# A norm of q and k cut into two chains, and an embedding norm that reads its statistics a tile ahead

## The reference

```python
# first block, inside attention: 4 heads, each with 2 x 64 features
q = rms_norm(q, g_q) * (HEAD_DK ** -0.5)     # over groups of 64 features
k = rms_norm(k, g_k)
# rms_norm(x, g) = x * rsqrt(mean(x * x) + EPS) * g
lam = exp(sum(lq[0] * lq[1])) - exp(sum(lq[2] * lq[3])) + lam_init
bias = bias_table[t5_buckets(kpos - qpos)]   # added to the scores
# after attention
x = x + gate1 * mix
h2 = rms_norm(x, g_norm2) * (1.0 + scale2) + shift2
# gate1, shift2, scale2 are parts of silu(c) @ w_mod + b_mod

# second block, its first line: a layer norm of every token
h = layer_norm(x, ln_emb_g, ln_emb_b)
```

## Time and profile before

| | |
|---|---|
| time, median of 3 | 2403.66 us (2400.92 to 2405.05) |
| profiled execution | 2396.91 us, span 2394.8 us |
| busy: PE / DVE / ACT / POOL | 90% / 73% / 44% / 7% of the span |
| mean granted TensorE clock | 0.932 of full speed |

### The profile page before, as it was taken

How to read it: one execution, slowest core, us unless ns; L and a number is a source line. 1 busy time by engine, 2 the same in 40 slices (tenths; PEclk the granted TensorE clock), 3 DMA queues, 4 the chain that set the end, 5 groups by cost and what they waited for, 6 DMA issues and landing times. The chain is left out here.

```text
span 2394.8 us, 25614 instructions
## 1 busy us (share of the span) xinstructions
PE 2146.2 (90%) x10172; PEld 1667.9 (70%) x10172; DVE 1744.9 (73%) x1857; ACT 1053.7 (44%) x1190; POOL 165.0 (7%) x122
## 2 busy tenths in 40 slices
PE   5999979999954999999999069999999969899997
PEld 3767824667843888888887047888888647788775
DVE  4565135997467799999997359999999469955737
ACT  4387022774224677777775022112221246522123
POOL 2000000000000011111110000000000000042210
PEclk8999986999976999999999569999999978899999
DMA  9111170001276899999997311121222140332201
GB/s 316 44 36 36 36 286 0 1 1 72 88 277 254 316 403 394 395 393 403 393 393 245 127 44 38 63 79 36 83 102 88 33 153 1 124 114 88 71 1 71
DMA packets 125719, 365.03 MB, mean 152 GB/s; under 512 B 11733, under 2 KB 22893, under 8 KB 125623
## 3 DMA queue, kind: packets, MB, share of 16 engines
q1 hardware_dynamic: 111616, 328.68, 36.1%
q0 software_dynamic: 6336, 21.00, 3.4%
q10 hardware_dynamic: 7670, 14.03, 1.6%
HBM read 324.76 MB, written 38.86 MB: 152 GB/s over the span
## 5 line engine op out<-in xcount | busy, mean ns | idle before, releaser
L2031 DVE SCALAR_TENSOR_TENSOR arena<-arena,vecs 128x1023 f32<-128x1023 f32 (+14 forms) x240 | 304.4, 1268 | 7.1
L1560 DVE TENSOR_TENSOR w_low<-W,w_high 128x2048 fp32r<-128x2048 f32 x96 | 217.0, 2287 | 38.9 <-ACT w_high L1512 38.9
L1928 PE MATMUL Q<-hT_high,w_high 128*128 128x512 f32 (+1 forms) x736 | 227.0, 391 | 5.9 <-DVE ring_low L2074 5.8
L1560 DVE TENSOR_TENSOR w_low<-arena,w_high 128x2048 fp32r<-128x2048 f32 x96 | 218.3, 2290 | 17.7 <-ACT w_high L1512 17.7
L1512 ACT ACTIVATE w_high<-W 128x2048 fp32r<-128x2048 f32 x96 | 184.0, 1919 | 96.6 <-PE Q L1455 65.3
L1928 PE MATMUL Q<-hT_low,w_high 128*128 128x512 f32 (+1 forms) x720 | 222.2, 390 | 0.0
L1928 PE MATMUL Q<-hT_high,ring_low 128*128 128x512 f32 x704 | 217.2, 390 | 0.0
L1512 ACT ACTIVATE w_high<-arena 128x2048 fp32r<-128x2048 f32 x96 | 184.2, 1919 | 74.9 <-PE Q L1455 74.9
L1455 PE MATMUL Q<-w_high,x_high 128*128 128x512 f32 x512 | 160.8, 395 | 2.4 <-DVE x_low L1563 2.4
L1928 PEld LDWEIGHTS Q<-hT_high,w_high 128*128 128x128 f32 (+1 forms) x736 | 135.4, 184 | 39.0 <-DVE ring_low L2074 5.9
L1455 PE MATMUL Q<-w_low,x_high 128*128 128x512 f32 x512 | 158.8, 391 | 0.0
(11 more groups left out here) (430 smaller groups left out, 4295.1 us busy)
## 6 DMA issues: line engine op xcount, KB each, us to landing
W<-in_w_dram SPq DMA_DIRECT2D x48, 2048.0 KB, 13.3
arena<-in_w_dram SPq DMA_DIRECT2D x48, 2048.0 KB, 12.3
W<-in_w_mod_dram SPq DMA_DIRECT2D x12, 2048.0 KB, 9.5
W<-in_w_in_dram SPq DMA_DIRECT2D x12, 2048.0 KB, 8.7
W<-in_w_out_dram SPq DMA_DIRECT2D x6, 2048.0 KB, 9.0
spill<-arena ACTq DMA_DIRECT2D x24, 512.0 KB, 2.6
W<-in_w_in_dram SPq DMA_DIRECT2D x8, 1024.0 KB, 7.7
arena<-in_x_dram SPq DMA_DIRECT2D x4, 1024.0 KB, 17.4
```

The lines of the kernel that those rows point to most:

```text
L1560: nc.vector.tensor_tensor(wl[:], chunk_src(r, j), wh[:].bitcast(F32), ALU.subtract).then_inc(low_v, 1)
L1928: ins = nc.tensor.matmul(Q[rows, 2 * (n % 4) + half, :], w[:, k], x[:, k, HALF * half:HALF * half + HALF], start=k == 0 and w is high and ...
L2031: ins = nc.vector.scalar_tensor_tensor(conf[:, i, j:], u[:, 0:S - j], w, conf[:, i, j:], ALU.mult, ALU.add)
```

## The change

In the block of q and k the 16 rows become two chains of 8 rows (`VECS = 2 * HEADS`), one for q (`g` = 0, partitions 0 to 7) and one for k (`g` = 1, partitions 64 to 71), each with its own sums, root (`root`), reciprocal (`invert`) and spread. The inverse roots are split: ScalarE writes the rounded high part (`high_rows`), VectorE the rest 32 partitions further on (`low_rows`), and one fp32r matmul over both spreads them with a rounded mask; the partitions between are zero. TensorE's list begins with a modulation product, the bias product moves behind the first two sums and the second modulation product, and the norms on VectorE use two bank pairs in place of four. The bias round trip goes to GpSimd's queue. `y_rest` moves to the end; the load of `gain2` and L937's operation move two blocks on, to the block of the output projection.

In the block of the embedding norm the tokens come in 8 DMAs of 0.5 MB, the 20 small loads go to GpSimd's queue, and `stats(t + 1)` is done ahead of the passes of tile `t`, in two sets of statistics; the copy of L1758 and a wait go.

```diff
+        VECS = 2 * HEADS
...
+        def rows_of(g):
+            return slice(DK * g, DK * g + VECS)
+
+        def rest_of(g):
+            return slice(DK * g + 32, DK * g + 32 + VECS)
...
+                for h in range(HEADS):
+                    pool.wait_ge(near_ready, h + 1)
+                    pool.dma_start(bias_rows[h].rearrange("(p n) -> p n", p=P), bias_near[h]).then_inc(bias_sent, 16)
+                pool.wait_ge(bias_sent, 16 * HEADS)
+                for h in range(HEADS):
+                    skewed = bias_rows[h, P:].rearrange("(p n) -> p n", n=HALF - 1)[:, 0:NEAR]
+                    pool.dma_start(bias_all[:, h, 6 * P:6 * P + NEAR], skewed).then_inc(bias_in, 16)
...
+                def next_vector(i):
+                    row_product(i)
+                    if i < 5:
+                        mod_product(pe, unit(pe, U_GATE1 + i + 1), 5)
+
+                def sums(g):
+                    for b in range(HEADS):
+                        n = HEADS * g + b
+                        pe.wait_ge(sq_ready, n + 1)
+                        for half in range(2):
+                            ins = nc.tensor.matmul(Q[rows_of(g), sum_bank[g] + half, :], qk_sum[:, b],
+                                                   tiles(n % 2)[:, HALF * half:HALF * half + HALF],
+                                                   start=b == 0, stop=b == HEADS - 1)
+                        ins.then_inc(sum_mm, 1)
+                        if b % 2:
+                            next_vector(2 * g + b // 2)
+                        if n == 1:
+                            near()
+
+                def spread(g):
+                    pe.wait_ge(parts_low, g + 1)
+                    span = slice(DK * g, DK * g + 32 + VECS)
+                    for b in range(HEADS):
+                        n = HEADS * g + b
+                        if n >= 2:
+                            pe.wait_ge(qk_normed, n - 1)
+                        for half in range(2):
+                            ins = nc.tensor.matmul(Q[:, 6 * (n % 2) + half, :], qk_spread[span, b],
+                                                   qk_parts[span, HALF * half:HALF * half + HALF],
+                                                   start=True, stop=True)
+                        ins.then_inc(spread_mm, 1)
+
+                def near():
+                    pe.wait_ge(hot_in, 16)
...
                 mod_product(pe, unit(pe, U_GATE1), 5)
-                for b in range(8):
-                    pe.wait_ge(sq_ready, b + 1)
-                    for half in range(2):
-                        ins = nc.tensor.matmul(Q[0:VECS, 6 + half, :], qk_sum[:, b],
-                                               tiles(b % 2)[:, HALF * half:HALF * half + HALF],
-                                               start=b == 0, stop=b == 7)
-                    ins.then_inc(sum_mm, 1)
-                    if b % 2:
-                        row_product(b // 2)
-                        mod_product(pe, unit(pe, U_GATE1 + b // 2 + 1), 5)
-                row_product(4)
-                mod_product(pe, unit(pe, U_GATE1 + 5), 5)
+                pe.wait_ge(lam_ready, 1)
+                nc.tensor.matmul(Q[:, 4, 0:2], ones[0:DK, :], lam_pr[0:DK, 0:2], start=True, stop=True)\
+                    .then_inc(lam_mm, 1)
+                pe.wait_ge(masks, 2)
+                sums(0)
+                pe.wait_ge(near_ready, HEADS)
+                sums(1)
+                next_vector(4)
+                pe.wait_ge(masks, 7)
+                pe.wait_ge(mask_ready, 1)
+                spread(0)
                 row_product(5)
-                pe.wait_ge(mod_added, 6)
-                pe.wait_ge(near_ready, HEADS)
-                pe.wait_ge(rows_inv, 1)
-                for b in range(8):
-                    if b >= 4:
-                        pe.wait_ge(qk_normed, b - 3)
-                    for half in range(2):
-                        ins = nc.tensor.matmul(Q[:, 2 * (b % 4) + half, :], qk_spread[:, b],
-                                               qk_rows[:, HALF * half:HALF * half + HALF], start=True, stop=True)
-                    ins.then_inc(spread_mm, 1)
+                spread(1)
...
+                def high_rows(g):
+                    act.wait_ge(rows_inv, g + 1)
+                    nc.scalar.activation(qk_parts[rows_of(g)], qk_rows[rows_of(g)], ACT.Copy).then_inc(parts_high, 1)
...
+                part(1)
+                root(0)
+                square(4)
+                square(5)
+                part(2)
+                square(6)
+                square(7)
+                act.wait_ge(masks, 7)
+                high_rows(0)
+                part(3)
+                root(1)
+                part(4)
                 for m in range(2):
                     nc.scalar.activation(y_high[m][:], y_lru[:, m], ACT.Copy).then_inc(ylru_high_ready, 1)
-                act.wait_ge(sum_mm, 8)
-                nc.scalar.activation(qk_rows, bank2(3)[0:VECS], ACT.Sqrt, bias=eps_col[0:VECS], scale=1.0 / DK)\
-                    .then_inc(root_q, 1)
-                for i in (4, 5):
-                    part(i)
+                part(5)
+                high_rows(1)
...
+                def invert(g):
+                    dve.wait_ge(root_q, g + 1)
+                    nc.vector.reciprocal(qk_rows[rows_of(g)], qk_rows[rows_of(g)]).then_inc(rows_inv, 1)
+
+                def low_rows(g):
+                    dve.wait_ge(parts_high, g + 1)
+                    nc.vector.tensor_tensor(qk_parts[rest_of(g)], qk_rows[rows_of(g)],
+                                            qk_parts[rows_of(g)].bitcast(F32), ALU.subtract).then_inc(parts_low, 1)
+
+                def norm(n):
+                    dve.wait_ge(spread_mm, n + 1)
+                    nc.vector.scalar_tensor_tensor(qk[:, n], qk[:, n], qk_gain[:, n // HEADS:n // HEADS + 1],
+                                                   bank2(3 * (n % 2)), ALU.mult, ALU.mult).then_inc(qk_normed, 1)
...
                 dve.wait_ge(mod_in, 4 * 16)
-                for i in range(4):
-                    added(i)
+                added(0)
+                for h in range(HEADS):
+                    dve.wait_ge(near_mm, h + 1)
+                    nc.vector.tensor_copy(bias_near[h], Q[:, h, :]).then_inc(near_ready, 1)
+                added(1)
+                invert(0)
+                added(2)
+                low_rows(0)
+                dve.wait_ge(near_ready, HEADS)
...
+                invert(1)
+                added(3)
+                added(4)
+                norm(0)
+                norm(1)
+                low_rows(1)
+                norm(2)
+                norm(3)
+                added(5)
+                for n in range(HEADS, 2 * HEADS):
+                    norm(n)
                 for m in range(2):
                     y_rest(dve, m)
...
-                dve.wait_ge(root_q, 1)
-                nc.vector.reciprocal(qk_rows, qk_rows).then_inc(rows_inv, 1)
-                for i in (4, 5):
-                    added(i)
-                dve.wait_ge(gain2_in, 16)
-                dve.wait_ge(mod_added, 6)
-                nc.vector.scalar_tensor_tensor(SCALE2, SCALE2, 1.0, gain2, ALU.add, ALU.mult).then_inc(scale_made, 1)
-                for b in range(8):
-                    dve.wait_ge(spread_mm, b + 1)
-                    nc.vector.scalar_tensor_tensor(qk[:, b], qk[:, b], qk_gain[:, b // 4:b // 4 + 1], bank2(b % 4),
-                                                   ALU.mult, ALU.mult).then_inc(qk_normed, 1)
...
+                sync.dma_start(gain2, bc_row(A["g_norm2"][0], D)).then_inc(gain2_in, 16)
                 sync.dma_start(tiles(16, 8), A["x"][0].rearrange("(t p) d -> p t d", p=P)).then_inc(x_again, 16)
...
                     add_mix(0, t)
+                dve.wait_ge(gain2_in, 16)
+                nc.vector.scalar_tensor_tensor(SCALE2, SCALE2, 1.0, gain2, ALU.add, ALU.mult).then_inc(scale_made, 1)
                 for k in range(KD // 2, KD):
                     out_rest(dve, 1, k)
+                dve.wait_ge(scale_made, 1)
...
-                for half in range(2):
-                    r0 = HALF * half
-                    sync.dma_start(xt[:, 4 * half:4 * half + 4],
-                                   tokens_acc[r0:r0 + HALF].rearrange("(t p) d -> p t d", p=P)).then_inc(xt_in[half], 16)
+                for t in range(NT):
+                    sync.dma_start(xt[:, t], tokens_acc[P * t:P * t + P]).then_inc(xt_in[t], 16)
...
+                pool.dma_start(dt_w[:], w_in2[:, COL_DT:COL_DT + SH].rearrange("(k p) e -> p k e", p=P),
...
-                act.wait_ge(small2_in, 16 * (4 + NT + len(rows)))
+                def root(t):
+                    act.wait_ge(emb_var, t + 1)
+                    nc.scalar.activation(rstd[:, t:t + 1], emb_mv[t % 2][:, 1:2], ACT.Sqrt, bias=eps5_col)\
+                        .then_inc(emb_root, 1)
+
+                root(0)
                 for t in range(NT):
```

(59 more changed lines are left out.)

95 lines of the change are left out of this document (39 added, 56 removed).

## The result

The changed kernel takes 2349.24 us (median of 4, 2347.2 to 2353.53) where the one before takes 2403.12: a ratio of 0.9778, 95% interval 0.9761 to 0.9795, so 53.9 us less. A second measurement, on its own, gave 0.9777 (0.9763 to 0.979), 53.5 us less. The forecast was 47.2 us less.

The account below looks back on a forecast made before the run. Bounds: the spread's pace in the block of q and k; in the embedding norm, ScalarE's late first root, then VectorE's period. 24.0 + 23.9 - 0.7 = 47.2 us off 2403.7 gives 2356.5 us, range 2346 to 2368.

Parts of the forecast that it names:

- part 1: Block of q and k: 84.2 us down to 60.2, a gain of 24.0 us, bounds 20 to 28.6.
- The idle time of TensorE: Block of q and k, before the fifth row product: TensorE idles about 5 us for VectorE's fourth addition.
- the row product behind it: Block of q and k: the fifth row product, after TensorE's wait for the fourth addition, 1.3 us.
- the modulation product: Block of q and k: the last modulation product, before the first spread, 3.64 us at the low clock.
- The allowance for the clock: Block of q and k: 2 us added for a clock that falls at the 32-row bias products and comes back.
- Part 2: Output projection: L937's 1.23 us now stands between the additions and the four splits; 0.7 us lost.
- Part 3: Embedding norm: first reciprocal 16.8 us earlier and 7.1 less up to the eighth; gain 23.9 us, bounds 20 to 26.
- The 0.2 a tile that I had left in: Embedding norm: the tile period was forecast to fall from 6.10 to about 5.45 us.
- The small loads: Embedding norm: 20 loads on GpSimd, 0.77 us each to issue, 6.2 to land, hidden by 22 us.
- The slower rival: Embedding norm: small loads on GpSimd at 4.5 us each eat part 1's gain; at 5.5 each, 2424. Chance 0.03.
- what the prediction names from the Trainium skill: GpSimd's small loads: a DMA issued from GpSimd starves while VectorE runs a copy in its two-port mode.
- The rival of a clock that stays up: Block of q and k: TensorE's clock does not fall, giving 2 + 2.6 us more: 2352. Chance 0.18.

Follow-up runs that it names:

- the fillers: Changed kernel with fourth addition, splits and L937's operation moved earlier, plus 13 unused 128-row products behind the spreads: 2341.47 us, ratio 0.9752 to the kernel before.
- the run with held loads: Changed kernel with fourth addition, splits and L937's operation moved, embedding tile loads from the third held until `emb_g` and `emb_b` landed: 2349.89 us, ratio 0.9789.

## Why the prediction was right

*The bound.* Both places were as read: the spread, and ScalarE's queue ahead of its first root. The runs with one of them undone cost 19.5 and 12.7 us.

*The steps of part 1.* Measured from the block's beginning, forecast in brackets: second addition 18.9 (19.0), first reciprocal 19.5 (19.7), second 32.3 (32.4), first norm 44.9 (45.5), end of the norms 56.7 (57.5), first score 59.3 (60.2). The idle time of TensorE was 6.35 (5), which is no term of the sum. Of the terms, the row product behind it was 2.05 (1.3) and the modulation product 2.46 (3.64); that they made up for each other is luck. A block's spread took 0.73 us where the clock was high, and two took 2.41 where it was low, so 1.2 each against the 0.9 of the forecast; both lie under the 1.28 of a norm, so VectorE set the pace as forecast. The allowance for the clock, 2 us, was 0.5 at the one-hot products and 1.3 at the sums behind; in another execution with the same instructions there it was 0.9 and 2.6. The bias round trip on GpSimd was through about 32 us after the block's beginning (36), hidden as forecast; but the prediction gave the move no gain, and undoing it costs 7.0 us. `b_mod` landed at 13.0 (13), and cost nothing. The reciprocals over 8 rows cost 6.53 and 6.54, what 16 rows cost.

*Part 2.* Forecast 0.7. TensorE stood still for 0.7 us, and VectorE's two additions around the place were 6.32 us apart instead of 5.44: 0.9.

*Part 3.* First reciprocal 10.8 after the block's beginning (10.5), period 5.24 (5.45), together 24.9 (23.9). The 0.2 a tile that I had left in are mainly two steps: the reciprocal starts 0.13 us after the aggregation has begun, less than the 0.21 that this takes, and the low part follows the second pass by 1.20 us instead of 1.32. The small loads took half the time to issue that I counted, but landed late. The changed kernel's DMA issues in this block, KB of each and us from issue to landing at the end:

```profile
arena<-in_b_glu_dram POOLq DMA_DIRECT2D x1, 8.0 KB, 14.9
small<-in_a_log_dram POOLq DMA_DIRECT2D x8, 0.1 KB, 5.9
```

14.9 us for the last against the 6.2 of the earlier trace rows; it was issued 12 us after the block's beginning and so there at 27 (28), and TensorE asked for it at 50. The slower rival was far off: its loads would have had to cost 4.5 us each, and they cost 0.5 to 1.0. VectorE ran statistics, a reciprocal and passes beside these issues and no copy, so what the prediction names from the Trainium skill (SBUF: State Buffer, on "DVE blocks DMA") is not put to the test here.

*The size.* 47.2 forecast, 53.9 and 53.5 measured, about 49 shown by the blocks. The range held it. The rival of a clock that stays up (2352) lies nearer to the time, but hasn't the cause, since the clock did fall at the one-hot products and again before the spread. The slip is 1.8 us in the blocks' terms (1.0 in each of them, less 0.2 at the projection); what else there is lies in the 4 us that no profile here places. A forecast from one profiled execution that lay 6 us under its median carries that error.

## What to carry to other kernels

A TensorE that is busy may still be slow: look at the granted clock beside the busy share, and ask what the clock does over products of few rows; here four lines that made them 128 rows tall gave 13.5 us, where the whole rewrite of that block gave 24.7. Twenty small loads ahead of an engine's first instruction are that engine's work; put them on an engine that has nothing to do. When one chain becomes two, look for the small step that the other engine needs and that stands behind the long one: here an addition of 0.7 us behind a reciprocal of 6.5 cost 4.3 us. And when a change moves a DMA to another queue, ask what stood behind it on the old one: here the weights came 17 us sooner.

## What the runs showed of the hardware

- 32 fp32 records took 27.67 us over 16 rows (clock 0.50) and 16.13 us over 128 rows (0.50, then 0.99), at the same place and with the same columns.
- The level that TensorE's clock has at the end of one block is carried into the next. In the two runs that end the block of q and k at 1.00 (the spread over 128 rows, the fillers), the scores of the attention took 160.7 us, with the clock of their first 20 us at 1.00. In the kernel before, the changed kernel and the run with held loads it is 0.50 at the end, and the scores took 165.9, 164.3 and 162.5 us, with 0.59, 0.64 and 0.89 in the first 20 us. How soon it rose again differed between executions of the same instructions: two further ones with the changed kernel's own instructions up to there took 162.4 us, with 0.89.
- A reciprocal over 1024 elements a row took 6.53 us over 8 rows and over 16.
- The load of `emb_b`, 0.5 MB broadcast from one row, landed in 8.9 us with all tiles asked for beside it, and in 8.9 us with two of the eight asked for.
